# The folded Fourier step of a two-block transformer kernel: sum and difference made on VectorE instead of in TensorE's accumulation

## What is computed

```python
def fourier_mix(u, w_f, b_f):
    ug = u.reshape(B, S, N_FGROUPS, FGROUP_DIM).astype(jnp.float32)
    f = jnp.fft.fft(ug, axis=3, norm='ortho')
    f = jnp.fft.fft(f, axis=1, norm='ortho').real.astype(u.dtype)
    y = jnp.einsum('bsgc,gcd->bsgd', f, w_f)
    return y.reshape(B, S, FOURIER_WIDTH) + b_f
# in each of the DEPTH = 2 layers:
    a = diff_attention(q, k, v, lam, lam_init, subln_g[l])
    f = fourier_mix(u, w_f[l], b_f[l])
    mix = jnp.einsum('bse,ed->bsd', jnp.concatenate([a, f], axis=-1), w_o[l])
```

## Time and profile before

| | |
|---|---|
| median of 3 runs | 943.79 us (943.78 to 944.28) |
| the profiled execution | 944.1 us, span 942.3 us |
| busy: TensorE (PE), its weight loads (PEld) | 917.8 us (97%), 772.1 us (82%) |
| busy: VectorE (DVE), ScalarE (ACT), GpSimd (POOL) | 622.3 us (66%), 474.9 us (50%), 129.8 us (14%) |
| mean granted TensorE clock | 0.996 |

### The profile page before, as it was taken

One profiled execution on the slowest core, in us unless ns is written; L12 is line 12 of the kernel. 1 busy time (PEld: TensorE's weight loads), 2 busy tenths in 40 slices (PEclk: granted clock), 3 DMA queues, 4 the chain that ended last, 5 costly groups with the idle time before them and its releaser, 6 DMA issues.

```text
span 942.3 us, 13528 instructions
## 1 busy us (share of the span) xinstructions
PE 917.8 (97%) x4998; PEld 772.1 (82%) x4998; DVE 622.3 (66%) x1073; ACT 474.9 (50%) x764; POOL 129.8 (14%) x100
## 2 busy tenths in 40 slices
PE   9999899999999999999999999999999999999996
PEld 6999788889888868888788888887978788888885
DVE  4798888776767777577774554557476864555545
ACT  5755656655686444673354343434575344434340
POOL 5553774201000010001100000000001100000001
PEclk9999999999999999999999999999999999999999
DMA  8754322364434217232565555543532255555521
GB/s 326 251 180 162 129 90 90 134 226 176 179 134 147 79 57 303 99 136 80 197 225 188 202 177 193 179 170 137 185 135 90 90 208 206 177 212 178 183 86 46
DMA packets 22236, 151.74 MB, mean 161 GB/s; under 512 B 2592, under 2 KB 2976, under 8 KB 4256
## 3 DMA queue, kind: packets, MB, share of 16 engines
q1 hardware_dynamic: 20160, 142.62, 42.5%
q10 hardware_dynamic: 2016, 8.29, 2.4%
HBM read 149.85 MB, written 1.05 MB: 160 GB/s over the span
## 4 chain that ended last, share of the span: by engine, by line
PE 83%; DVE 10%; ACT 3%; issue 3%; POOL 1%; POOLq 0%; DVEq 0%; ACTq 0%
PE ps L509 15%; PE ps L515 15%; PE ps L511 15%; PE ps L1112 5%; PE ps L540 3%; PE ps L544 3%; PE ps L542 3%; PE ps L788 2%; DVE wlo L1762 2%; PE ps L790 2%; PE ps L789 2%; PE ps L560 2%; PE ps L1130 2%; PE ps L576 1%; PE ps L679 1%
## 5 line engine op out<-in xcount | busy, mean ns | idle before, releaser
L1293 ACT CAST whi<-raw 128x2048 fp32r<-128x2048 f32 x127 | 241.9, 1912 | 146.2 <-PE ps L515 112.1
L1762 DVE TENSOR_TENSOR wlo<-raw,whi 128x1024 fp32r<-128x1024 f32 x127 | 172.3, 1358 | 140.2 <-ACT whi L1293 139.9
L509 PE MATMUL ps<-whi,ahi 128*128 128x512 f32 (+2 forms) x448 | 173.6, 387 | 0.8 <-issue 0.6
L511 PE MATMUL ps<-wlo,ahi 128*128 128x512 f32 (+2 forms) x448 | 171.8, 383 | 0.0
L515 PE MATMUL ps<-whi,alo 128*128 128x512 f32 (+2 forms) x448 | 170.7, 384 | 0.0
L1768 DVE TENSOR_TENSOR wlo<-raw,whi 128x1024 fp32r<-128x1024 f32 x106 | 129.1, 1218 | 0.0
L509 PEld LDWEIGHTS ps<-whi,ahi 128*128 128x128 f32 x448 | 84.2, 188 | 18.4 <-issue 2.5
L511 PEld LDWEIGHTS ps<-wlo,ahi 128*128 128x128 f32 x448 | 84.2, 188 | 16.5 <-issue 0.5
L515 PEld LDWEIGHTS ps<-whi,alo 128*128 128x128 f32 x448 | 84.2, 188 | 16.3
L540 PE MATMUL ps<-ahi,whi 128*128 128x256 f32 x256 | 73.4, 287 | 0.0
L542 PE MATMUL ps<-alo,whi 128*128 128x256 f32 x256 | 72.4, 283 | 0.0
(11 more groups left out here) (284 smaller groups left out, 1737.1 us busy)
## 6 DMA issues: line engine op xcount, KB each, us to landing
raw<-in_wstream SPq DMA_DIRECT2D x134, 1024.0 KB, 4.8
par<-in_params ACTq DMA_DIRECT2D x5, 1024.0 KB, 4.8
tab<-in_tables ACTq DMA_DIRECT2D x1, 1370.0 KB, 7.5
res<-in_x SPq DMA_DIRECT2D x2, 512.0 KB, 4.6
out<-res SPq DMA_DIRECT2D x4, 256.0 KB, 2.1
par<-in_params ACTq DMA_DIRECT2D x1, 512.0 KB, 3.7
arena<-in_wf ACTq DMA_DIRECT2D x2, 256.0 KB, 5.1
arena<-in_wsmall ACTq DMA_DIRECT2D x1, 256.0 KB, 8.6
```

Of the source, the lines that this page charges most:

```text
L509: pe.matmul(banks[b][:, 0:cw], h_, wh[:, i, c], start=st, stop=False, skip_group_check=True)
L511: pe.matmul(banks[b][:, 0:cw], h_, wl[:, i, c], start=False, stop=False, skip_group_check=True)
L1293: act.copy(whi[:, u % SPL, :], raw[:, u % RAW, :]).then_inc(w_hi, 1)
L1762: dve.tensor_tensor(wlo[:, u % SPL, c], raw[:, u % RAW, c], whi[:, u % SPL, c].bitcast(F32), ALU.subtract).then_inc(w_lo_v, 1)
```

## The change

The four `fy` products become two, each started and stopped by itself: `cw[:, 0]` by the cosine part into columns 0 to 128 of the bank, `cw[:, 1]` by the sine part into columns 256 to 384. The negated weights go, and their place in SBUF becomes the ring `fyr` of finished rows; the ring `fbr` of copied sine parts lies where the attention rows `od` are written later. ScalarE copies the sine part (`f_part`). VectorE adds cosine part, bias and sine part to positions 0 to 128 and, reading both backward, takes cosine part plus bias minus sine part for positions 129 to 255 (`fourier_sum`, `f_sum`). ScalarE rounds the row from SBUF (`fourier_hi`), and VectorE subtracts it from the row (`fourier_lo`).

```diff
--- before.py
+++ after.py
@@ -358,6 +358,8 @@
         od = arena[:, 10240:11264].rearrange("p (t c) -> p t c", t=T)
         osq = arena[:, 11264:11776]
         wfs = arena[:, 12800:13312]
+        fyr = arena[:, 12800:13312].rearrange("p (r c) -> p r c", r=2)
+        fbr = arena[:, 10240:10240 + 2 * HF].rearrange("p (r c) -> p r c", r=2)
         sgr = arena[:, 0:1024].rearrange("p (r t c) -> p r t c", r=2, t=T)
         hfr = arena[:, 1024:2048].rearrange("p (r t c) -> p r t c", r=2, t=T)
         xsum = arena[:, 2048:4096].rearrange("p (t c) -> p t c", t=T)
@@ -407,7 +409,7 @@
         ds_psum, ds_max, dp_done, da_done = sem("ds_psum"), sem("ds_max"), sem("dp_done"), sem("da_done")
         do_psum, do_ss, do_rs, do_done = sem("do_psum"), sem("do_ss"), sem("do_rs"), sem("do_done")
         f_full, f_copied, fy_hi, fy_lo = sem("f_full"), sem("f_copied"), sem("fy_hi"), sem("fy_lo")
-        f_fold, cw_done = sem("f_fold"), sem("cw_done")
+        f_fold, cw_done, f_part, f_sum = sem("f_fold"), sem("cw_done"), sem("f_part"), sem("f_sum")
         lam_exp = sem("lam_exp")
         lam_pre = sem("lam_pre")
         lam_done = sem("lam_done")
@@ -1118,7 +1120,7 @@
 
                     if h == 0:
                         pe.wait_ge(qk_done, 4 * l + 2)
-                        pe.wait_ge(cw_done, 3 * l + 3)
+                        pe.wait_ge(cw_done, 2 * l + 2)
                     if h == NH // 2:
                         pe.wait_ge(qk_done, 4 * l + 4)
                     if h >= 1:
@@ -1150,11 +1152,9 @@
                     else:
                         pe.wait_ge(f_copied, NG * l + copied_count(g))
                         gc = slice(g * GD, (g + 1) * GD)
-                        for out, ws, at in ((bank[:, 0:HF], (cw[:, 0, gc], cw[:, 1, gc]), slice(0, HF)),
-                                            (bank[:, HF:S], (cw[:, 0, gc], wfs[:, gc]), slice(HF - 2, 0, -1))):
-                            for q in range(2):
-                                mm = pe.matmul(out, ws[q], pqr[:, g % 2, q, at], start=(q == 0), stop=(q == 1),
-                                               skip_group_check=True)
+                        for q in range(2):
+                            mm = pe.matmul(bank[:, q * S:q * S + HF], cw[:, q, gc], pqr[:, g % 2, q, 0:HF],
+                                           start=True, stop=True, skip_group_check=True)
                     mm.then_inc(f_full, 1)
 
                 def diff_pt(h):
@@ -1626,7 +1626,6 @@
                 for q in range(2):
                     act.wait_ge(f_fold, 2 * l + q + 1)
                     act.copy(cw[:, q, :], X[q]).then_inc(cw_done, 1)
-                act.activation(wfs, X[1], ACT.Identity, scale=-1.0).then_inc(cw_done, 1)
                 if l == 0:
                     load_par(2)
                     load_par(3)
@@ -1669,8 +1668,11 @@
                         act.copy(pqr[:, g % 2, :, 0:HF], FB[g].rearrange("p (q k) -> p q k", q=2)[:, :, 0:HF]
                                  ).then_inc(f_copied, 1)
                     else:
-                        act.activation(bhi[:, 4 + g, :], FB[g][:, 0:S], ACT.Identity,
-                                       bias=vcol("b_f", 4 * l + g)).then_inc(fy_hi, 1)
+                        act.copy(fbr[:, g % 2, :], FB[g][:, S:S + HF]).then_inc(f_part, 1)
+
+                def fourier_hi(g):
+                    act.wait_ge(f_sum, NG * l + g + 1)
+                    act.copy(bhi[:, 4 + g, :], fyr[:, g % 2, :]).then_inc(fy_hi, 1)
 
                 def diff_pt_out(h):
                     f = FILL["dpt", l, h]
@@ -1690,6 +1692,9 @@
                         fourier_out(kind, g)
                     if h + 1 < NH:
                         probs(2 * h + 3)
+                    for kind, g in fourier_steps(h):
+                        if kind == "fy":
+                            fourier_hi(g)
                     if h >= 1:
                         diff_pt_out(h - 1)
                     if h == 0:
@@ -2318,11 +2325,21 @@
                                                        ALU.mult, ALU.add)
                     ins.then_inc(da_done, 1)
 
+                def fourier_sum(g):
+
+                    dve.wait_ge(f_part, NG * l + g + 1)
+                    bias = vcol("b_f", 4 * l + g)
+                    a, b = FB[g], fbr[:, g % 2, :]
+                    dve.scalar_tensor_tensor(fyr[:, g % 2, 0:HF], a[:, 0:HF], bias, b[:, 0:HF], ALU.add, ALU.add)
+                    back = slice(HF - 2, 0, -1)
+                    dve.scalar_tensor_tensor(fyr[:, g % 2, HF:S], a[:, back], bias, b[:, back],
+                                             ALU.add, ALU.subtract).then_inc(f_sum, 1)
+
                 def fourier_lo(g):
+
                     dve.wait_ge(fy_hi, NG * l + g + 1)
-                    dve.scalar_tensor_tensor(blo[:, 4 + g, :], FB[g][:, 0:S], vcol("b_f", 4 * l + g),
-                                             bhi[:, 4 + g, :].bitcast(F32), ALU.add, ALU.subtract
-                                             ).then_inc(fy_lo, 1)
+                    dve.tensor_tensor(blo[:, 4 + g, :], fyr[:, g % 2, :], bhi[:, 4 + g, :].bitcast(F32), ALU.subtract
+                                      ).then_inc(fy_lo, 1)
 
                 scores_max(0)
                 scores_max(1)
@@ -2331,9 +2348,12 @@
                         scores_max(2 * h + 2)
                     for kind, g in fourier_steps(h):
                         if kind == "fy":
-                            fourier_lo(g)
+                            fourier_sum(g)
                     if h + 1 < NH:
                         scores_max(2 * h + 3)
+                    for kind, g in fourier_steps(h):
+                        if kind == "fy":
+                            fourier_lo(g)
                     if h < NH:
                         combine(h)
 
```

## The result

| | before | changed |
|---|---|---|
| median, us | 944.22 (943.78 to 944.52, 5 runs) | 950.40 (948.11 to 951.09, 5 runs) |
| ratio | | 1.0055, 95% interval 1.0045 to 1.0066 |
| profiled execution, time / span, us | 944.1 / 942.3 | 950.44 / 948.7 |
| mean granted clock | 0.996 | 0.994 |
| matmul records | 4998 | 4966 |

The account below looks back on a forecast made before the run. Around `w_o`, the ScalarE-VectorE chain sets the time and TensorE is early. Per layer 1.90 us at `w_o` plus 0.09 at the transposes, 4.0 us in two layers, give 947.8 us against a 943.8 median; range 945.8 to 951.0.

Parts of the forecast that it names:

- The chain through VectorE: Ahead of `w_o`, two handover links become four: `combine(7)` 0.85 us later, `w_o` 1.90 us later per layer.
- The new wait at the transposes: Behind `w_o`, group 3's longer chain delays the attention rows' scaling; 0.09 us of new TensorE wait per layer.
- The likeliest case: The forecast itself, 947.8 us, with the granted clock at 1.00 from 425 to 435; chance 0.51 with its bounds.
- B: TensorE's clock falls behind the two waits ahead of `w_o`, 1.7 us lost: 949.5 in one layer, 951.2 both; chance 0.20.
- The removed products: `fy` steps: groups 0 to 2 give nothing; group 3's 0.44 us is used up at the transposes.
- Rival A: TensorE is the bound after all, so every removed `fy` product counts: 3.6 us less, 940.2; chance 0.06.
- Rival C: VectorE's backward-read difference costs 0.476 us instead of 0.34, three times a layer: 0.8 us more, 948.6; chance 0.12.
- Rival D: TensorE's 1.06 us idle at the norm takes up part of the delay: 945.7; chance 0.11 with similar slack.
- The negated copies: Two copies on ScalarE, 0.61 us each, removed; give nothing because ScalarE later waits 6.60 us for a DMA.

Follow-up runs that it names:

- the first experiment: Changed kernel with matmuls without use put into TensorE's two waits, ahead of head 7's turn and ahead of `w_o`: 947.71 us.
- before, delayed: Kernel before with idle VectorE operations ahead of `combine(7)` (0.85 us) and the remainder of group 1 (1.05 us): 949.68 us.
- the third experiment: Changed kernel with the sum of group 1 made right behind `combine(7)`, ahead of the two weight remainders: 950.37 us.
- the second new order: Changed kernel with VectorE doing `combine(7)` first, then groups 0 and 1, weight remainders in gaps in and behind the attention rows' scaling: 943.35 us.

## Why the prediction was right, and where it was not

**The chain through VectorE: right.** The steps from 422.02 on were given to 0.05 us. Counted from the cast, the sum was expected at 2.11 and came at 2.11, the remainder at 3.23 and 3.19, `combine(7)` at 3.57 and 3.53, `w_o` at +1.90 and +1.85. The kernel before with only a delay put in showed the same, +1.95.

**The new wait at the transposes: the term that was mis-sized.** The wait came, but the slack ahead of it had been read from the wrong row. The 438.22 of the earlier trace rows is a weight load (PEld), which runs beside the last product; the first transposing matmul started at 438.45, 0.23 us later. Behind a wait the two start together (kernel with both waits filled):

```profile
440.27 0.85 PEld L562 LDWEIGHTS ps<-tab,arena 128*128 128x128 f32 x8 [0.53 <-DVE arena L2383]
440.27 1.09 PE L562 MATMUL ps<-tab,arena 128*128 128x128 f32 x8
```

So the slack was 0.60 us, not 0.37, and the term comes out as 0.09 - 0.23 = -0.14. With the clock held at 1.00 the first transposing matmul stood 11.33 us behind `w_o`, 0.13 less than the 11.46 of before; from there to the turn behind the norm it took 13.36 us where it took 13.30. The layers' totals were 1.77 and 1.71, not 1.99, and the chain made 3.5 us of the forecast's 4.0.

**The clock: the step that failed.** The likeliest case had the granted clock at 1.00 from 425 to 435, and gave B a chance of 0.20 with 951.2 for both layers. B is what happened: both waits came out as worked out (1.86 and 1.69 us against 1.9 and 1.7), and half speed followed in both layers, at 1.43 and 1.58 us where 1.7 was the estimate. What was wrong was the weight. I placed the new case between two rows of before, one followed by a fall and one not, as if each were a fixed answer; the traces show the first of them to go either way, in kernels whose program is the same up to there. The range held the 950.40 because it took B in, and the main case's 947.8 is what was measured with both waits filled (947.71), not for the change as it stands. The rule from the Trainium skill, page "TensorE: Matmul & The Clock Gate", Part 1, by which idleness sends TensorE back to 1.2 GHz, is borne out by the first experiment: only the matmuls in the waits differ, the granted clock stays at 1.00, and the 3.0 us are gone from the marks.

**The removed products: right, with one thing unseen.** Those of groups 0 to 2 gave nothing and those of group 3 their 0.42 and 0.45 us. That they also kept TensorE busy between the waits was only in B's arithmetic and not in the part on costs: with them in place both waits stayed under 1.3 us and the clock stayed up in the profiled execution.

**Rival A** is refuted by the same run. **Rival C**: the difference, read backward, took 0.340 us for 127 columns beside 0.351 for the 129 of the sum. The Trainium skill's figure for small non-adjacent steps ("Vector Engine (DVE) Microarchitecture Reference", section 5.2), from which an estimate of 0.18 us more came, does not apply to the step of minus one here; the measurement decides. In all, the difference costs the 0.34 us that the sum had, not the 0.476 of the rival. **Rival D**: the delay went through the norm whole. From the first transposing matmul to the norm's first statistics on VectorE it took 8.40 us where it took 8.33, and TensorE's matmuls idled 1.05 us ahead of the turn behind the norm in both kernels.

**The negated copies**: no place was found where they counted.

## What to carry to other kernels

Fewer products on the busiest engine give nothing when the next product waits for another engine's chain; a link added to that chain costs its full length, and the order of that engine's queue (what can wait behind the chain) was worth more here than the products. A wait on TensorE has a second price, the clock behind it: add it to the sum as its own term when two waits come close together, and look whether work that is to be removed had kept them short. Where executions of one kernel lie 2 us apart, look for a wait whose fall of the clock comes and goes, and fill it before small differences are measured.

## What the hardware showed that was not expected

- The same wait gives different clocks. 2.50 us without a matmul in the scan were followed by half speed for 0 (changed kernel), 3.4 (before) and 6.8 us (before, delayed), and the cast 300 us later came at 420.03, 420.22 and 421.77. In the third experiment the same waits, 1.86 us and work, were followed by no fall in layer 0 and a fall in layer 1.
- A fall in the scan costs less than the work it holds up. 3.4 us at half speed hold up 1.7 us of work, 6.8 us hold up 3.4. From the end of the wait to the cast the first cost 0.7 us (304.5 to 304.6 against 303.8 to 303.9), the second 1.8 to 2.2 (305.7 to 306.1). VectorE is busy 5.93 of 6.00 us from 114 to 120 in the windows of the changed kernel above, so a part is probably hidden behind it; that was not tested.
- A weight load starts ahead of its matmul when nothing holds it: 438.22 against 438.45 in the kernel before, both at 440.27 behind a wait. The idle time of the loads is therefore longer than that of the matmuls, 1.36 against 0.94 us at the transposes of the second new order. A slack on TensorE is read from the matmul's row.
- VectorE read 127 columns of two inputs with a step of minus one in 0.340 us, where 129 columns forward took 0.351.
